# Up stage with split weights kept in HBM for the second 1024 tokens, token sums formed early, and first down tiles made in the last up unit

## The reference

```
h = RMSNorm(x);  q,k,v,p = h @ W_in
a = sliding-window attention(q,k,v);  m = multi-scale pooling(p)
x = x + concat(a, m) @ W_out
h2 = RMSNorm(x)
u = h2 @ W_up                       (1024 -> 2 x 2816)
c = causal depthwise conv(3) over tokens of u;  gate, val = split(c)
x = x + (silu(gate) * val) @ W_down   (2816 -> 1024)
```

## Time and profile before

| | us |
|---|---|
| median of 3 runs | 1975.93 (1974.67 to 1975.96) |
| the profiled execution | 1974.65 |
| its span, first to last instruction | 1972.6 |
| TensorE busy | 1804.4 (91%) |
| TensorE weight loads busy | 1490.8 (76%) |
| VectorE busy | 1357.4 (69%) |
| ScalarE busy | 880.0 (45%) |
| GpSimd busy | 267.4 (14%) |

### The profile page before, as it was taken

How to read it: one execution, slowest core, us unless ns; L and a number is a source line. 1 busy time by engine, 2 the same in 40 slices (tenths; PEclk the granted TensorE clock), 3 DMA queues, 4 the chain that set the end, 5 groups by cost and what they waited for, 6 DMA issues and landing times.

```text
span 1972.6 us, 23469 instructions
## 1 busy us (share of the span) xinstructions
PE 1804.4 (91%) x8490; PEld 1490.8 (76%) x8490; DVE 1357.4 (69%) x1805; ACT 880.0 (45%) x1520; POOL 267.4 (14%) x286
## 2 busy tenths in 40 slices
PE   6789889889874899999997799999999899999999
PEld 5668778778763688888886588888887688888887
DVE  4465445444532798988988789898897577774774
ACT  5453663663544444444444444444443433333331
POOL 1212201201102200000002200000000212220110
PEclk9989999999987899999998799999999899999999
DMA  5232253243443124222231222322223799885884
GB/s 178 65 128 65 65 189 122 75 154 104 165 155 121 57 68 139 75 86 87 74 96 54 85 93 68 97 75 86 86 75 102 267 364 330 291 294 148 293 284 143
DMA packets 214803, 271.39 MB, mean 138 GB/s; under 512 B 12249, under 2 KB 123553, under 8 KB 214689
## 3 DMA queue, kind: packets, MB, share of 16 engines
q1 hardware_dynamic: 195249, 215.37, 34.6%
q10 hardware_dynamic: 19440, 54.53, 7.1%
HBM read 221.62 MB, written 48.23 MB: 137 GB/s over the span
## 4 chain that ended last, share of the span: by engine, by line
PE 78%; DVE 7%; ACT 7%; DMA 3%; issue 3%; POOL 2%; SPq 0%; ACTq 0%; DVEq 0%; POOLq 0%
PE ps L535 25%; PE ps L536 25%; PE ps L537 25%; ACT xs L877 2%; DMA h2T_d<-hs 1%; DVE va_lo L1284 1%; ACT junk L789 1%; PE ps L573 1%; ACT n L801 1%; DVE cb L1330 1%; DMA x_d<-r 1%; ACT r L909 1%; POOL vs L1520 1%; ACT w_hi L771 1%; DVE w_lo L1098 1%
## 5 line engine op out<-in xcount | busy, mean ns | idle before, releaser
L535 PE MATMUL ps<-va_hi,wv_hi 128*128 128x512 f32 x1232 | 485.8, 394 | 56.2 <-DVE va_lo L1284 44.4
L536 PE MATMUL ps<-va_lo,wv_hi 128*128 128x512 f32 x1232 | 484.1, 393 | 0.0
L537 PE MATMUL ps<-va_hi,wv_lo 128*128 128x512 f32 x1232 | 483.6, 393 | 0.0
L535 PEld LDWEIGHTS ps<-va_hi,wv_hi 128*128 128x128 f32 x1232 | 234.3, 190 | 108.3 <-DVE va_lo L1284 46.7
L537 PEld LDWEIGHTS ps<-va_hi,wv_lo 128*128 128x128 f32 x1232 | 234.1, 190 | 49.7
L536 PEld LDWEIGHTS ps<-va_lo,wv_hi 128*128 128x128 f32 x1232 | 234.4, 190 | 48.6
L535 PE MATMUL ps<-dt_hi,ds_hi 128*128 128x512 f32 x616 | 244.3, 397 | 12.1 <-DVE ds_lo L1434 12.0
L536 PE MATMUL ps<-dt_lo,ds_hi 128*128 128x512 f32 x616 | 243.9, 396 | 0.0
L537 PE MATMUL ps<-dt_hi,ds_lo 128*128 128x512 f32 x616 | 243.7, 396 | 0.0
L1330 DVE SCALAR_TENSOR_TENSOR cb<-ub,cst,cb 128x1024 f32<-128x1024 f32 x176 | 221.9, 1302 | 7.4 <-ACT cb L969 7.4
L1098 DVE TENSOR_TENSOR w_lo<-raw,w_hi 128x1024 fp32r<-128x1024 f32 x72 | 96.3, 1347 | 135.3 <-ACT w_hi L771 134.8
(11 more groups left out here) (153 smaller groups left out, 2935.2 us busy)
## 6 DMA issues: line engine op xcount, KB each, us to landing
dg<-gT_d SPq DMA_DIRECT2D x264, 256.0 KB, 4.7
rw<-in_w_up_dram SPq DMA_DIRECT2D x88, 512.0 KB, 5.1
dw<-in_w_down_dram SPq DMA_DIRECT2D x132, 256.0 KB, 5.1
gT_d<-cb ACTq DMA_DIRECT2D x44, 512.0 KB, 2.6
raw<-in_w_in_dram SPq DMA_DIRECT2D x40, 512.0 KB, 3.8
raw<-in_w_out_dram SPq DMA_DIRECT2D x32, 512.0 KB, 3.9
n<-in_x_dram SPq DMA_DIRECT2D x16, 512.0 KB, 5.7
x_d<-r ACTq DMA_DIRECT2D x16, 512.0 KB, 3.2
```

The lines of the kernel that those rows point to most:

```text
L535: pe.matmul(out_ap, l_hi, r_hi, start=first, stop=False, skip_group_check=True)
L536: pe.matmul(out_ap, l_hi, r_lo, start=False, stop=False, skip_group_check=True)
L537: return pe.matmul(out_ap, l_lo, r_hi, start=False, stop=last, skip_group_check=True)
```

## The change

- The split weights of units 0 to 21 (both parts, 512 KB a product) are stored to a tensor `wS_d` in HBM as they are made (`keep_w`), and units 22 to 43 load them (`bring_w`) instead of making them. `load_rw`, `t13`, `t2_`, `t4`, `hi`, `lo` end with unit 21. `wv_hi` and `wv_lo` become the two halves of a slot of one tensor `wv`.
- GpSimd forms the token sums of half 1 in units 6 and 12 (`sums`), each kept apart, and SP stores them to `sT_d` (`keep_sums`, 512 KB each, 8 stores).
- In unit 21 all seven token combinations of half 1 are made whole, 128 x 2048 at once (`vv_hi`, `vv_lo`), from a 2-buffer `vv` that SP fills (`bring_v`, 1 MB each, the buffer of two before being free).
- In the last unit `t_hi`/`t_lo` of the first 5 weight tiles stand before `c11` on ScalarE and before `u3` on VectorE, and `s_hi`, `s_lo` of the first 3 token tiles after; the last unit's taps, `tanh`, `glu1`, `glu2` and store move into the first 6 down steps.
- `ds_hi` and `ds_lo` move by 0.125 KiB to 70.125 and 80.125; `res0` and `res1` swap places, and their loads wait for less.

```diff
+        sT_d = nc.dram_tensor("sT_d", [4, 2, P, 2, T], F32, kind="Internal").ap()
+        wS_d = nc.dram_tensor("wS_d", [FT, NP, P, 2, 4 * P], F32, kind="Internal").ap()
...
+        vv = at("vv", 0, [P, 2, 4, T])
-        wv_hi, wv_lo = at("wv_hi", 52.125, [P, WSLOTS, 4 * P], F32R), at("wv_lo", 70.125, [P, WSLOTS, 4 * P], F32R)
+        wv = at("wv", 52.125, [P, WSLOTS, 2, 4 * P], F32R)
+        wv_hi, wv_lo = wv[:, :, 0, :], wv[:, :, 1, :]
-        ds_hi, ds_lo = at("ds_hi", 70, [P, SSLOTS, T], F32R), at("ds_lo", 80, [P, SSLOTS, T], F32R)
+        ds_hi, ds_lo = at("ds_hi", 70.125, [P, SSLOTS, T], F32R), at("ds_lo", 80.125, [P, SSLOTS, T], F32R)
...  SP
+            def keep_w(un):
+                for i in range(NP):
+                    n = NP * un + i
+                    sp.wait_ge(S["u_lo"], n + 1)
+                    sp.dma_start(wS_d[un, i], as_f32(wv[:, n % WSLOTS])).then_inc(w_kept[n % WSLOTS], 16)
+            def bring_w(un, i):
+                n, kept = NP * un + i, NP * (un - FT) + i
+                wait(sp, "prod", n - WSLOTS + 1)
+                ...
+                sp.dma_start(as_f32(wv[:, n % WSLOTS]), wS_d[un - FT, i]).then_inc(w_in[n % WSLOTS], 16)
+            def bring_v(i):
+                wait(sp, "vv_lo", i - 1)
+                ...
+            keep_w(0)
             load_rw(1)
             next_chunk(1)
-            for un in range(2, N_UP):
-                load_rw(un)
+            for un in range(1, FT):
+                keep_w(un)
+                if un + 1 < FT:
+                    load_rw(un + 1)
                 (un == 4: load_vs(2, j); 7: keep_sums(0); 10: load_vs(3, j); 13: keep_sums(1); 16: bring_v(0), bring_v(1))
+            for un in range(FT, N_UP):
+                for i in range(NP):
+                    bring_w(un, i)
+                    if un == FT and i >= 2:
+                        bring_v(i)
...  ScalarE, up(un)
+                if un == FT - 1:
+                    vv_hi(0)
                 if un:
                     tanh(un - 1)
+                if un == FT - 1:
+                    vv_hi(1)
...
+                if un == N_UP - 1:
+                    for tau in range(T_EARLY):
+                        t_hi(tau)
                 act.wait_ge(S["prod"], NP * un + 5)
                 wait(act, "glu1", un)
                 a_.activation(ub[:, 0, 2:2 + T], ps[:, bank0, :], ACT.Copy).then_inc(S["c11"], 1)
...  VectorE, up(un)
+                if last:
+                    for tau in range(T_EARLY):
+                        t_lo(tau)
                 dve.wait_ge(S["prod"], NP * un + 4)
                 ...
                 v.tensor_tensor(ub[:, 1, h1], ps[:, bank0 + 3, :], k1[:], ALU.add).then_inc(S["u3"], 1)
...  VectorE, down
+                if i == 1:
+                    taps(N_UP - 1)
+                if i == 4:
+                    glu1(N_UP - 1)
+                    glu2(N_UP - 1)
...  GpSimd
+            def sums(n):
+                (waits for the four loads of vs, then four tensor_tensor of 128x1024, each after the one before)
             for un in range(N_UP):
+                if un == 6:
+                    sums(2)
+                if un == 12:
+                    sums(3)
                 bring_halo(un)
                 keep_halo(un)
```

More of the change, by code:

```diff
@@ L293, in bass_hybrid_block @@
             "tanh glu1 g_ready g_out halo_in halo_kept ub_clear "
-            "t_added t_hi t_lo s_added s_hi s_lo d_used d_done y_added stored").split()}
+            "vv_hi vv_lo s_kept t_added t_hi t_lo s_added s_hi s_lo d_used d_done y_added stored").split()}
         x_in = [sem(f"x_in{t}") for t in range(NT)]
@@ L341, in v_source_wait, with vv_landed @@
                 wait(engine, {1: "s1", 2: "s2", 3: "s3", 5: "s4"}[i], v + 1)
+        def vv_landed(i):
+            return 16 * sum(1 if j in (0, 4, 6) else 2 for j in range(i % 2, i + 1, 2))
         def tile_used(sigma):
@@ L983, in up @@
                 bank0 = 4 * (un % 2)
[L984 to L989, removed]
+                if un == 0:
+                    for i in range(NP):
+                        v_hi(1, i)
                 if un:
                     tap2(un - 1, 0)
-                if head:
-                    for i in range(3, NP):
-                        v_hi(v, i)
                 hi(un + 1, 0)
@@ L1021, in up @@
                 a_.activation(ub[:, 0, 2:2 + T], ps[:, bank0, :], ACT.Copy).then_inc(S["c11"], 1)
-                if tail:
-                    v_hi(v + 1, 4)
+                if un == FT - 1:
+                    vv_hi(4)
                 hi(un + 1, 6)
+                if un == N_UP - 1:
+                    for sigma in range(S_LEAD):
+                        s_hi(sigma)
                 tap2(un, 1)
-                if tail:
-                    v_hi(v + 1, 5)
-                    v_hi(v + 1, 6)
+                if un == FT - 1:
+                    vv_hi(5)
+                    vv_hi(6)
             act.wait_ge(S["h2_copied"], KT * NB)
@@ L1044, in t_hi @@
                 else:
[L1045 removed]
+                    wait(act, "prod", NP * (N_UP - 1) + (2 if tau < 7 else 3))
                 if t_loads(tau) == 2:
@@ L1341, in glu2, with taps @@
                                        ).then_inc(S["g_ready"], 1)
+            def taps(un):
+                tap(un, 1, 1)
+                tap(un, 0, 1)
+                tap(un, 1, 0)
+                tap(un, 0, 0)
             def up(un):
                 bank0 = 4 * (un % 2)
[L1345 to L1347 removed]
+                switch, last = un == FT - 1, un == N_UP - 1
                 h0, h1 = slice(2, 2 + T), slice(2 + T, 2 + 2 * T)
[L1349 to L1351 removed]
+                if un == 0:
+                    for i in range(NP):
+                        v_lo(1, i)
                 if un:
[L1353 to L1359 removed]
+                    taps(un - 1)
                 t13(un + 1)
@@ L1363, in up @@
                 v.tensor_tensor(k1[:], ps[:, bank0 + 1, :], k1[:], ALU.add).then_inc(S["u2"], 1)
+                if switch:
+                    vv_lo(0)
                 t2_(un + 1)
```

212 lines of the change are left out of this document (118 added, 94 removed).

## The result

| | before | changed |
|---|---|---|
| median, the two run beside each other | 1975.93 us (1973.67 to 1976.69, 5 runs) | 1987.63 us (1984.09 to 1992.22, 5 runs) |
| span of the profiled execution | 1972.6 | 1982.3 |

The ratio is 1.0059 (95% interval 1.0039 to 1.0078): slower by 0.6%. The prediction said 1959 us and faster; the time lies outside its range of 1944 to 1981, near the rival *Stores bind* (1990), which had a chance of 0.11.

A forecast was written before the change was run, and what follows sets the result against it. TensorE never rests inside up and down, so only what keeps it waiting or slows its stream counts. 1974.65 - 25 + 7 + 13 - 1 - 10.5 = 1958.2, median 1.3 above, given as 1959 us; range 1944 to 1981.

The forecast's parts named there:

- Stores bind: Half 0 of up: rw pair lands over 10 us after the last `lo`; stores cost 38, not 7; 1990 us; chance 0.11.
- Part 2: Units 0 to 21: stores of split weights ahead of the rw loads make each unit 0.3 us late; cost 7 us.
- The estimate from the Trainium skill's figure of 358 GB/s: Same stores at 1.46 us each: the loop 1.5 us late a unit, cost about 29 us, time 1981.
- Part 1: Switch from unit 21 to 22: 11.4 us lost instead of 36.5, with waits of 2.8, 4.2 and 2.3; gain 25 us.
- Part 3: Units 6 and 12: GpSimd's sums hold up VectorE and delay `u3`, 6.5 us a unit; cost 13 us.
- Part 4: Start of down: the stall moves before product 6 of the last unit, 11.6 us plus 2.4 of low clock; gain 1.
- Part 5: Down: moving ds by 128 bytes brings 443 instead of 432 matmuls in 100 us; gain 10.5 us, little certainty.

## Why the prediction was wrong

**What failed is one term, the cost of the stores in Part 2.** It was put at 7 us and is 29.8. The mechanism, its place and its consequence stand as written: the rw pair hangs behind the last `lo`, `t13` is late, `u3` is late, product 6 waits. The sizes of the steps: the stores were to be through 4.8 us after the last `lo`, and the first load packets start at 4.8, so the row of the single gT_d store was the right one for a stream of them too (1.28 us for 512 KB against 1.3). The pair was then to take 3.84 us, and `t13` starts 5.1 after its first packets. Most of that miss could be read before: alone, with no store near, a pair needs some 4.6 us from its first packet to its landing, and 3.84 is only the share of the window in which the DMA engines were busy for it. With 4.6 the same sum gives 9.4 us, 1.1 late a unit instead of 0.3. The rest, about 0.5, goes with the change from stores to loads, where the rate falls; that part is an estimate from unit 20, and no run took the change away alone. In a loop with 8.33 us of room, a miss of 1.3 us is the whole difference between 0.3 and 1.6 us late, and it comes in each of 20 units.

How much of the loss is the stores' depends on what is taken away first. The table gives them 29.8 us and the sums 12.9. With the loads ahead, the c21 rows gave 26 back and left 16 for the sums. The total, 42.7 where 20 was forecast, is the same, and so is the step that failed.

The *Stores bind* rival was the nearest, but its reason was wrong: it let the stores run at 1.52 us, and they don't. Its 1990 is close to 1987.63 by luck, as its cost of 38 was 8 us too high, and the switch, the start of up and the scatter of the runs made up for it.

The estimate from the Trainium skill's figure of 358 GB/s (DMA: Bandwidth & Descriptors, Specifications) was a cost of about 29, and 29.8 came. That too is luck: it rested on 1.46 us a store, and the trace has the stores at 411 GB/s and 1.28 us. The delay came behind them.

**The error of judgement** is that bounds of 0 and 38 us stood around the term, the value was taken near the lower one from rows that left out what was new, stores and loads back to back, and the upper one got 0.11. The prediction even states that nothing else in the loop is slack.

**Part 1, the switch**: gain 22.1 for 25. The stalls were forecast as 2.8, 4.2 and 2.3 us, and are 1.83, 6.34 and 2.59, in the forecast places. In all 14.5 us are lost instead of 11.4. The long one goes with the chain of loads: from the issue of a 1 MB load to the start of its high part it took 4.6, 7.5, 7.4, 6.8 and 5.7 us, where 5.1 was taken.

**Part 3, the sums**: 13 forecast. Units 6 and 12 are 6.5 us longer than their late neighbours, 12.9 for both, and spreading the sums gave 12.9 back in the medians. By the c21 rows of the kernel with the loads ahead they are 8 us longer than 19.04 each, 16 in all, so the agreement with 6.5 a unit is in part luck.

**Part 4, the start of down**: the stall moved in front of product 6 of the last unit as forecast. VectorE and TensorE there:

```profile
1554.18 0.69 DVE L1498 TENSOR_TENSOR dt_lo<-dtw,dt_hi 128x512 fp32r<-128x512 f32 x1 [2.59 <-ACT dt_hi L1124]
1554.79 0.68 DVE L1472 TENSOR_TENSOR ub<-ps,k 128x512 f32<-128x512 f32 x1
...
1555.62 0.77 PE L605 MATMUL ps<-va_hi,wv 128*128 128x512 f32 x1 [12.28 <-DVE ub L1472]
```

The wait is 12.28 us for 11.6, the unit 13.9 us longer for 14.0, and down then starts at once and without a starved step.

**Part 5, the place of ds**: forecast 10.5 with little certainty; the edit alone gave 9.1, and 443 matmuls. Together Parts 4 and 5 were to give 11.5, and the table has 25.4 - 13.9 = 11.5.

So by the table four of the five parts hold within 3 us, and the sum misses by 26.2 in the profiled execution: 22.8 for the stores, 2.9 for the switch, 0.5 at the start of up. The median of the runs lies 3.5 us above the profiled one, where 1.3 was allowed. The changed kernel scatters over 8 us and the one before over 3 in five runs each, but over 6 and 8 in its larger groups, so that is no mark of the change.

## What to carry to other kernels

- A transfer that a loop waits for goes into its queue ahead of transfers that nobody waits for. Here the order alone is worth 29 us, 1.5%.
- When a loop's room is within a few tenths of its load, the cost is not the small difference but the error of the terms, times the number of rounds: give the far end of the range the chance it has.
- A busy share times its window is what a transfer costs the DMA engines, not how long its reader waits. For a wait take the time from its first packet to its landing: 4.6 us here where the busy share gave 3.84.
- Two engines that exclude each other cost nothing where one of them waits for a third anyway: put GpSimd's sum there. A tile queued early in front of an addition that frees a PSUM bank is paid by the matmuls behind that bank.

## What the runs showed of the hardware

- Where the stationary and the moving operand lie in a partition sets the pace of fp32r matmuls of 128x512: they start 0.232 us apart (432 in 100 us) when the operands lie a multiple of 512 bytes and 128 more apart, 0.229 (439) at 64 more, 0.227 (443) at none. I had not expected the step between.
- DMA stores of 4 KB packets: 411 GB/s, 160 ns a packet. Where loads of 512-byte packets follow them: 229 GB/s for 2 us at a DMA share of 0.94, with the last store packets at 295 ns for the most part. In the kernel with the loads ahead, where stores follow loads, store packets keep to 160 ns to the last.
- VectorE's operations with two SBUF inputs and GpSimd's don't overlap: an addition of 128x1024 takes 3.40 us instead of 1.23 beside a GpSimd one, a tap 2.31 instead of 1.27 beside one of 128x512, and GpSimd's own take 3.26 instead of 2.40 and 1.60 instead of 1.30.
